# Expert layer: the second token tile takes half of its experts by fetched rows and VectorE additions

## The chip, the cores and the metric

The kernel is one program on one core of a Trainium2 chip. The metric is the device time of one launch in microseconds, the median of the runs shown. The profile is one more execution, recorded by the hardware profiler.

## The reference, cut to what matters

A model of one token sequence (256 tokens, 2048 features, everything float32): a block with a recurrent and a sparse-attention branch, then an expert layer, then two more layers. The change touches the expert layer alone:

```
s = q . sub_keys                       # 8 heads, two halves of 128 keys each
s1, i1 = top_k(s[0], 16); s2, i2 = top_k(s[1], 16)
top_s, pos = top_k(all 256 sums s1 + s2, 16)        # 16 experts a head, 128 a token
eid = i1 * 128 + i2                    # one of 16384 experts
gate = softmax(top_s)
act = gelu(x . expert_u[eid])
out = sum over the token's 128 experts of gate * act * expert_v[eid]
```

Each expert has a row u and a row v of 2048 numbers. A token uses 128 of the 16384.

## The kernel before, in words

**Weights.** All weights of the program come through one stream of units of 128x2048 float32 (1 MB), which SyncE loads into a ring of four slots (`ring`). ScalarE rounds each unit to `hi_w` in two halves (`split_hi`, L216 and L217), and VectorE or GpSimd subtracts to get `lo_w` (`split_lo`, L222 and L224), so that a float32 product becomes three fast ones (hi.hi, hi.lo, lo.hi) on TensorE. A slot is loaded again when TensorE has used its unit (semaphore `unit_used`).

**Dense evaluation.** The layer doesn't pick experts. It evaluates all 16384 for all 256 tokens, 128 experts to a unit: all those with the same second index i2. A u unit (`u_unit`) gives 128 experts x 256 tokens into a PSUM bank (16 steps of three 256-column products), ScalarE takes gelu of it into `GG`. A dense table G of gates (zero where a token doesn't use an expert) is multiplied in, and a v unit (`v_unit`) multiplies the result, again split in hi and lo (`high`, L2212, and `low`, L2392), by v: for two token tiles of 128 and four column blocks of 512, three products each, 24 matmuls of 512 columns (L2074), summed over all units in PSUM.

**Order.** The experts go in two halves of 64 units: u0, v0, u1, v1. For each half x is rebuilt and added to (`x_added`, L2511). In u1 a paired form is used for 60 of the 64 units: one 512-column product for hi_w with both halves of x (L2043) and one of 256 columns (L2045), which VectorE sums (`u_sum`, L2348) ahead of gelu.

**The gate table.** In units 0 to 36 of u0 VectorE finds the 16 best of each list; from unit 40 on, 32 bursts of TensorE (`burst`, L2059) build G for 8 tokens each out of one-hot tables, which VectorE builds (`build`, L2356 and L2357) and ScalarE scales (`gate`, L2217). One half of a burst's result is multiplied into `GG` (`product`), the other is staged to memory (`stage`, tensor `other_G`) and read back in u1 (`load_back`, `product_back`).

**Who splits.** GpSimd does `split_lo` for the first 40 units of u0 and nothing else in this layer; VectorE does all the others. The order on every engine is written out by hand, as program text of that engine; SyncE's queue carries the stream, the table and the saved x in one order.

Of the kernel before, what the change touches and what calls it, by code (L numbers as in the profile page):

```python
# [13 lines left out]
P = 128  # L14
# [38 lines left out]
STREAM = [("w_in", 19), ("br_b", 2), ("br_a", 2), ("w_out", 4), ("wq", 4), ("u0", 16), ("v0", 16), ("u1", 16), ("v1", 16),  # L53
# [6 lines left out]
GROUPS = _g  # L60

# [9 lines left out]
def constants():  # L71
# [10 lines left out]
    c["iota"] = f(t)  # L82
    c["anti"] = f(u + t == P - 1)
# [32 lines left out]
def build(nc, dram, consts):  # L116
# [1786 lines left out]
    HK = PK // 2  # L1903
# [3 lines left out]
    GG = sb("GG", (P, T, HK))  # L1907
# [18 lines left out]
    gg = lambda i: GG[:, :, i]  # L1926
# [4 lines left out]
    other_G = scratch("other_G", (P, T, HK))  # L1931
    back = [h[:].rearrange("p a q c -> p (a q c)").rearrange("p (n i) -> p n i", i=HK) for h in (hot1, hot2)]
    kept = x[:].rearrange("p t d -> p (t d)")
# [9 lines left out]
    W0, A0 = GROUP["u0"] * SLOTS, GROUP["a_in"] * SLOTS  # L1943
    EARLY = 3
    tile = lambda tt: slice(tt * P, (tt + 1) * P)
    V_ORDER = ([(tt, c) for tt in range(NT) for c in range(4)], [(tt, c) for c in range(4) for tt in range(NT)])
    NB, NK = T // 8, T // 32
    U_AT, V_AT = (0, 2 * HK), (HK, 3 * HK)
    ROUTED, STEADY = 37, (36, 48)
    AT = [40 * KC + 364 * j // NB for j in range(NB)]  # L1950
    AT_UNIT = [at // KC for at in AT]
    PAIRED = HK - SLOTS
    at_unit = lambda i: [j for j in range(NB) if AT_UNIT[j] == i]
    AT_CHUNK = [48 + 2 * k for k in range(NK)]
    LATE = [[], []]
    for hf, (marks, n) in enumerate(((AT_UNIT, 8), (AT_CHUNK, 32))):
        at = 0
        for m in marks:
            LATE[hf].append((m, at))
            at += n * (HK - m)  # L1960
        assert at <= NT * D

    def rest(hf, j):

        (m, at), n = LATE[hf][j], (8, 32)[hf]
        return m, kept[:, at:at + n * (HK - m)].rearrange("p (n i) -> p n i", n=n)

    with nc.Block() as block:  # L1968
        @block.sync
        def _(sp):  # L1970
# [8 lines left out]
            cload(sp, iota[:], "iota", S("sk_in"))  # L1979
            sp.dma_start(x_saved, x[:]).then_inc(S("x_out"), 16)  # L1980
# [4 lines left out]
            def refill_unit(w):  # L1985
                g, s = divmod(w, SLOTS)
                sp.wait_ge(S("unit_used"), W0 + w + 1)
                sp.dma_start(ring[s][:], wst[GROUP["u0"] * SLOTS + SLOTS + w]).then_inc(S(f"landed{s}"), 16)

            def load_back(k):  # L1990
                sp.dma_start(back[k % 2], other_G[:, 32 * k:32 * k + 32, :]).then_inc(S(f"back{k % 2}"), 16)

            u0, v0 = GROUP["u0"], GROUP["v0"]
            refill(u0, STEADY[0] // SLOTS)
            for i in range(STEADY[0], HK):
                refill_unit(i)
                for j in at_unit(i):
                    sp.wait_ge(S("staged"), j + 1)
                    sp.dma_start(other_G[:, 8 * j:8 * j + 8, :], staged[:, j % 2]).then_inc(S(f"other_out{j % 2}"), 16)
            refill(v0, 4)  # L2000
            sp.wait_ge(S("late"), NB)
            sp.dma_start(x[:], x_saved).then_inc(S("x_again"), 16)
            refill(v0 + 4, 12)
            u1, v1 = GROUP["u1"], GROUP["v1"]
            refill(u1, 2)
            sp.wait_ge(S("x_added"), 8)
            sp.dma_start(x_saved, x[:]).then_inc(S("x_out"), 16)
            refill(u1 + 2, STEADY[1] // SLOTS - 4)
            for p in range(2):
                sp.wait_ge(S(f"other_out{p}"), 16 * (NB // 2))  # L2010
            load_back(0)
            refill(u1 + STEADY[1] // SLOTS - 2, 1)
            load_back(1)
            refill(u1 + STEADY[1] // SLOTS - 1, 1)
            for i in range(STEADY[1], HK):
                refill_unit(2 * HK + i)
                if i in AT_CHUNK[:NK - 2]:
                    k = AT_CHUNK.index(i)
                    sp.wait_ge(S("back_used"), k + 1)
                    load_back(k + 2)  # L2020
            refill(v1, 4)
            sp.wait_ge(S("late"), NB + NK)
            sp.dma_start(x[:], x_saved).then_inc(S("x_again"), 16)
            for dst, name in ((gcol[:], "a_norm_w"), (gcol2[:], "norm_final_w")):
                sp.dma_start(dst, dram[name]).then_inc(S("xa_col"), 16)
            sp.wait_ge(S("back_used"), NK)
            sp.dma_start(fgain[:], bcast("norm_final_g")).then_inc(S("fgain"), 16)
            refill(v1 + 4, 12)
# [5 lines left out]
        def _(t):  # L2034
            def u_unit(g, s, hf, paired, between=()):
                t.wait_ge(S("gelu_free"), g * 4 + (hf * HK + s + 1))
                t.wait_ge(S(f"lo{s}"), g + (GROUP[f"u{hf}"] + 1))
                for k in range(KC):
# [3 lines left out]
                    if paired:  # L2042
                        nc.tensor.matmul(PS[:, s, :].rearrange("p (a c) -> p a c", a=2), hi_w[s][:, k * P:(k + 1) * P], both_x[:, :, k, :],  # L2043
                                         start=k == 0, stop=False)
                        m = nc.tensor.matmul(PS[:, s, 0:T], lo_w[s][:, k * P:(k + 1) * P], hi_x[:, k, :], start=False, stop=k == KC - 1)  # L2045
                        continue
# [1665 lines left out]
```

## Time and profile before

| what | us |
|---|---|
| median of 3 runs (3487.63 to 3488.38) | 3488.04 |
| span of the profiled execution, first to last instruction | 3487.5 |
| TensorE busy in it | 3450.4 (99%) |
| VectorE busy | 2194.8 (63%) |
| ScalarE busy | 1766.6 (51%) |
| GpSimd busy | 347.2 (10%) |
| first and last product of the expert layer (u0 to v1) | 924.5 to 2424.5 |

Busy time is the union of an engine's instructions. Matmuls are pipelined, so a matmul's duration (0.39 us for 512 columns) is longer than the distance of two starts (0.23 us); what a unit costs is read from starts. Engines in rows: PE is TensorE, PEld its weight loads, DVE VectorE, ACT ScalarE, POOL GpSimd, SP SyncE; a q behind the name is that engine's sequencer.

### The profile page before, as it was taken

Reading aid. Unit: us, or ns where it says so; the run is one execution under the profiler, and the core shown is the slowest. Engines: PE = TensorE matmul, PEld = TensorE weight load, DVE = VectorE, ACT = ScalarE, POOL = GpSimd, SP = SyncE. Lnnn points to the kernel's source line nnn. Section 1 sums busy time; section 2 is a strip of 40 time slices with the busy share of each in tenths; the row PEclk is TensorE's granted clock in tenths of the full one; section 3 lists DMA queues with packets and bytes.
Section 4 is the critical chain, followed back from the end, with each engine's and each line's share of the span. In section 5 each row is a group of like instructions: output and inputs, shape, how many; then the busy total and the mean of one; then the engine's idle time right before and its main releaser. Section 6 shows DMA issues by size and latency. Waiting matters only on the chain. (4 is left out here: it accounts for less than half of the span.)

```text
span 3487.5 us, 50169 instructions
## 1 busy us (share of the span) xinstructions
PE 3450.4 (99%) x20098; PEld 2893.0 (83%) x20098; DVE 2194.8 (63%) x2937; ACT 1766.6 (51%) x2613; POOL 347.2 (10%) x215
## 2 busy tenths in 40 slices
PE   8999999999999999999999999999999999999999
PEld 7777777787999998888888888887788877788887
DVE  4777765765666686555555565555788885555454
ACT  5563444334444785444444444444655654444863
POOL 0000000000499100000000000000122210000000
PEclk9999999999999999999999999999999999999999
DMA  6554533565445555555555666555543435455444
GB/s 235 203 198 156 174 138 130 187 232 212 161 183 182 174 168 183 215 190 185 191 213 184 240 231 228 189 185 180 191 148 138 148 140 202 168 194 190 145 150 164
DMA packets 111214, 638.58 MB, mean 183 GB/s; under 512 B 17770, under 2 KB 23690, under 8 KB 39224
## 3 DMA queue, kind: packets, MB, share of 16 engines
q1 hardware_dynamic: 106696, 622.98, 50.0%
q0 software_dynamic: 4336, 13.14, 1.2%
q8 instruction: 119, 1.95, 0.2%
q14 instruction: 63, 0.52, 0.0%
HBM read 611.10 MB, written 21.54 MB: 181 GB/s over the span
## 5 line engine op out<-in xcount | busy, mean ns | idle before, releaser
L222 DVE TENSOR_TENSOR lo_w<-ring,hi_w 128x1024 fp32r<-128x1024 f32 x500 | 612.4, 1225 | 862.7 <-ACT hi_w L216 854.2
L216 ACT CAST hi_w<-ring 128x1024 fp32r<-128x1024 f32 x540 | 567.1, 1050 | 946.3 <-DMA ring<-in_wstream 920.6
L224 DVE TENSOR_TENSOR lo_w<-ring,hi_w 128x1024 fp32r<-128x1024 f32 x500 | 612.4, 1225 | 0.0
L217 ACT CAST hi_w<-ring 128x1024 fp32r<-128x1024 f32 x540 | 564.4, 1045 | 0.0
L639 PE MATMUL PS<-hi_w,both_x 128*128 128x512 f32 (+2 forms) x1520 | 500.2, 399 | 4.9 <-DVE RKV L1651 3.0
L2074 PE MATMUL PS<-hi_w,hi_g 128*128 128x512 f32 x1024 | 404.0, 395 | 2.0 <-issue 2.0
L2667 PE MATMUL PS<-hi_w,both_x 128*128 128x512 f32 x1232 | 401.3, 401 | 4.1 <-PEq L1968 1.9
L2074 PE MATMUL PS<-lo_w,hi_g 128*128 128x512 f32 x1024 | 403.4, 394 | 0.0
L2074 PE MATMUL PS<-hi_w,lo_g 128*128 128x512 f32 x1024 | 403.2, 394 | 0.0
L2048 PE MATMUL PS<-both_x,hi_w 128*128 128x256 f32 x2176 | 390.5, 281 | 3.1 <-POOL lo_w L224 3.1
L639 PEld LDWEIGHTS PS<-hi_w,both_x 128*128 128x128 f32 x1520 | 285.2, 189 | 78.3 <-issue 12.3
L2048 PEld LDWEIGHTS PS<-both_x,hi_w 128*128 128x128 f32 x2176 | 334.9, 189 | 3.5 <-ACT GG L2291 3.4
L2043 PE MATMUL PS<-both_x,hi_w 128*128 128x512 f32 x960 | 336.0, 393 | 0.0
L2048 PE MATMUL PS<-both_x,lo_w 128*128 128x256 f32 x1088 | 307.1, 282 | 0.0
L639 PE MATMUL PS<-lo_w,both_x 128*128 128x512 f32 (+2 forms) x760 | 293.1, 386 | 0.0
L2667 PEld LDWEIGHTS PS<-hi_w,both_x 128*128 128x128 f32 x1232 | 231.9, 188 | 61.2 <-DVE x L3035 2.8
L2045 PE MATMUL PS<-both_x,lo_w 128*128 128x256 f32 x960 | 270.5, 282 | 0.0
L3182 PE MATMUL PS<-hi_w,both_x 128*128 128x512 f32 x768 | 247.4, 398 | 0.0
L2667 PE MATMUL PS<-lo_w,both_x 128*128 128x512 f32 x616 | 241.4, 392 | 0.0
L2074 PEld LDWEIGHTS PS<-hi_w,hi_g 128*128 128x128 f32 x1024 | 192.7, 188 | 46.7 <-issue 2.2
L2074 PEld LDWEIGHTS PS<-hi_w,lo_g 128*128 128x128 f32 x1024 | 192.1, 188 | 45.8
L2074 PEld LDWEIGHTS PS<-lo_w,hi_g 128*128 128x128 f32 x1024 | 192.1, 188 | 44.3
(579 smaller groups left out, 5272.4 us busy)
## 6 DMA issues: line engine op xcount, KB each, us to landing
ring<-in_wstream SPq DMA_DIRECT2D x540, 1024.0 KB, 4.8
other_G<-staged SPq DMA_DIRECT2D x32, 256.0 KB, 6.0
hot<-other_G SPq DMA_DIRECT2D x8, 1024.0 KB, 7.0
gates_dram<-gst POOLq DMA_DIRECT2D x8, 512.0 KB, 4.6
x_dram<-x SPq DMA_DIRECT2D x2, 2048.0 KB, 11.8
x<-x_dram SPq DMA_DIRECT2D x2, 2048.0 KB, 9.3
prev<-RKV POOLq DMA_DIRECT2D x6, 508.0 KB, 5.1
x<-in_x SPq DMA_DIRECT2D x4, 512.0 KB, 8.9
```

The costliest lines, as they stand in the source:

```text
L216: a.copy(hi_w[s][:, 0:HALF], ring[s][:, 0:HALF]).then_inc(S(f"hi{s}"), 1)
L217: a.copy(hi_w[s][:, HALF:UNIT], ring[s][:, HALF:UNIT]).then_inc(S(f"hi{s}"), 1)
L222: v.tensor_tensor(lo_w[s][:, 0:HALF], ring[s][:, 0:HALF], hi_w[s][:, 0:HALF].bitcast(F32), ALU.subtract)
L224: v.tensor_tensor(lo_w[s][:, HALF:UNIT], ring[s][:, HALF:UNIT], hi_w[s][:, HALF:UNIT].bitcast(F32), ALU.subtract)\
L639: mm = nc.tensor.matmul(PS[:, bank(m, tt), 0:n], xa[:, xo + kk_, tt * P:(tt + 1) * P], wa[slot][:, k * 512:k * 512 + n], start=(kk_ == 0 a ...
L2043: nc.tensor.matmul(PS[:, s, :].rearrange("p (a c) -> p a c", a=2), hi_w[s][:, k * P:(k + 1) * P], both_x[:, :, k, :], start=k == 0, stop=F ...
L2045: m = nc.tensor.matmul(PS[:, s, 0:T], lo_w[s][:, k * P:(k + 1) * P], hi_x[:, k, :], start=False, stop=k == KC - 1)
L2048: m = nc.tensor.matmul(PS[:, s, 0:T], wa[s][:, k * P:(k + 1) * P], xa[:, k, :], start=(k == 0 and p == 0), stop=(k == KC - 1 and p == 2))
L2074: m = nc.tensor.matmul(PS[:, 4 * tt + c, :], ga[:, s, tt * P:(tt + 1) * P], wa[s][:, c * 512:(c + 1) * 512], start=first and p == 0, stop= ...
L2667: mm = nc.tensor.matmul(o, xa[:, kk, tt * P:(tt + 1) * P], wa[q][:, k * 512:(k + 1) * 512], start=(kk == 0 and p == 0), stop=(kk == KC - 1 ...
L3182: mm = nc.tensor.matmul(PS[:, 2 * (m % 2) + tt, :], xa[:, kk, tt * P:(tt + 1) * P], wa[q][:, k * 512:(k + 1) * 512], start=(kk == 0 and p ...
```

## The change

- The stream is reordered: 64 u units (`u_b`, i2 below 64), 64 u units (`u_a`), then 128 v units. All 128 u units use the form with three 256-column products.
- Token tile 0 goes as before. Token tile 1 uses dense products for the 64 expert blocks of `u_a` only. For the blocks of `u_b` its 128 selected experts are taken one slot at a time: GpSimd fetches by indirect DMA, for each of the 128 tokens, the 8 KB row of v of its expert in slot s (`fetch`, out-of-range indices, those of the other half, are skipped), and VectorE adds row times weight to x (`add_row`, 128x2048, with a drain). The activation of that expert and token is fetched by 128 more indirect DMAs of one element per token (`cell`), out of a copy of all activations of `u_b` in memory (`act_dram`, written by SyncE in `keep_act`).
- So 64 v units are dense (24 matmuls, `v_dense`) and 64 are half (12 matmuls, tile 0 alone, `v_half`): six dense, then half and dense in turn, then six half (`v_expert`).
- 54 additions stand in `u_a` (one a unit from the tenth on), 74 in the first 119 of the 128 v units. Rows go through three or four buffers; a fetch waits until the addition that used its buffer is done.
- GpSimd does `split_lo` for all 64 units of `u_b` and for every second unit of v; VectorE for `u_a` and for the other half of v. In `u_a` GpSimd issues 128 cells and its fetches.
- VectorE's products with `GG` (`product`, `late`, `product_back`, `u_sum`) go; in their place come `copied`, `times_a` (128x256, one a unit of `u_a`) and `times_b` (128x128, one a half unit). The table for `u_b` is loaded in one DMA of 4 MB ahead of the refills of the v units.

```
+HK = PK // 2
+LEAD = 6
+def v_expert(p):
+    if p < LEAD:
+        return False, p
+    if p >= 2 * HK - LEAD:
+        return True, p - HK
+    k = (p - LEAD) // 2
+    return ((p - LEAD) % 2 == 0, k) if (p - LEAD) % 2 == 0 else (False, LEAD + k)
...
+    ADD0, ADDS_U = 10, HK - 10
+    ADDS_V = PK - ADDS_U
+    SPAN_V = LAST_A - 2
+    adds_u = lambda i: [i - ADD0] if i >= ADD0 else []
...
+    fetch_tick = {s: add_tick[row_before[s]] + 1 if row_before[s] >= 0 else (ADD0 if s < 3 else add_tick[s] - 6) for s in range(PK)}
...
+            def keep_act(w):
+                s = w % SLOTS
+                sp.wait_ge(S("gelu_free"), w + 5)
+                sp.dma_start(act_dram[w], act_stage(w)).then_inc(S(f"act_out{s}"), 16)
...
+            sp.dma_start(tab_b, other_G).then_inc(S("tab_in"), 16)
+            for p in range(VB):
+                refill_unit(VB + p)
+                sparse, k = v_expert(p)
+                if sparse and k + AHEAD < HK:
+                    load_act(k + AHEAD)
...
+            def v_half(g, s, last=False):
+
+                t.wait_ge(S(f"lo{s}"), g + (GROUP["v"] + 1))
+                t.wait_ge(S("g_lo"), g * 4 + (s + 1))
+                for c in range(4):
+                    m = v_products(g, s, 0, c, False, last)
...
+            for p in range(VB):
+                if p + 2 < VB:
+                    high(p + 2)
+                hi(VB + p + SLOTS - 1)
...
         @block.gpsimd
         def _(g):
-            for w in range(AT_UNIT[0]):
+            def fetch(s):
+
+                n = row_of[s]
+                if row_before[s] >= 0:
+                    g.wait_ge(S("added"), row_before[s] + 1)
...
+                g.indirect_dma_start(rows[n], None, dram["v_rows"], bass.IndirectOffsetOnAxis(ap=row_at[:, s:s + 1], axis=0),
+                                     bounds_check=HK * P - 1, oob_is_err=False).then_inc(S(f"row_{n}"), 16)
+
+            def cell(s):
+
+                g.indirect_dma_start(raw[:, s:s + 1], None, act_cells, bass.IndirectOffsetOnAxis(ap=cell_at[:, s:s + 1], axis=0),
+                                     bounds_check=HK * P * T - 1, oob_is_err=False).then_inc(S(f"cells{s // CELLS}"), 16)
...
+            for w in range(HK):
+                lo(w)
+                if w == 48:
+                    g.wait_ge(S("row_at"), 1)
+                    fetch(0)
+            for s in (1, 2):
+                fetch(s)
+            for s in range(SLOTS):
+                g.wait_ge(S(f"act_out{s}"), 16 * (HK // SLOTS))
+            for s in range(2 * CELLS):
+                cell(s)
+            for i in range(ADD0, HK):
+                for s in fetches(i):
+                    fetch(s)
+                at = 2 * CELLS + 4 * (i - ADD0)
+                for s in range(at, min(at + 4, PK)):
+                    cell(s)
+            lo(VB)
+            lo(VB + 2)
+            for p in range(VB):
+                for s in fetches(HK + p):
+                    fetch(s)
+                if p % 2 and p + SLOTS - 1 < VB:
+                    lo(VB + p + SLOTS - 1)
...
+            def add_row(s):
+
+                n = row_of[s]
+                if s == 0:
+                    v.wait_ge(S("x_again"), 16)
+                v.wait_ge(S(f"row_{n}"), 16 * row_turn[s])
+                v.scalar_tensor_tensor(out=x1, in0=rows[n], scalar=weight[:, s:s + 1], in1=x1, op0=ALU.mult, op1=ALU.add)
+                v.drain().then_inc(S("added"), 1)
...
+            for i in range(HK):
+                lo(HK + i + SLOTS - 2)
+                if i:
+                    times_a(i - 1)
+                if i in (9, 12, 36, 38):
+                    weigh((9, 12, 36, 38).index(i))
+                for s in adds_u(i):
+                    add_row(s)
...
+            for p in range(VB):
+                if p + 3 < VB and v_expert(p + 3)[0]:
+                    times_b(v_expert(p + 3)[1])
+                    v.drain()
+                if p + 2 < VB:
+                    low(p + 2)
+                if p < VB - 1:
+                    lo(VB + p + SLOTS - 1)
+                for s in adds_v(p):
+                    add_row(s)
```

## Rows read from the trace of the kernel before

**Rows 1.** Stages u0 (two parts), v0, u1, v1: busy time of each engine.
```profile
core 0: us, PE busy (x) PEld busy (x) DVE busy (x) ACT busy (x) POOL busy (x), PEclk, DMA share, GB/s
924.50:1155.00 230.50, 227.45 (x1921) 227.05 (x1920) 149.49 (x419) 107.34 (x138) 200.15 (x76) 1.00 0.50 178
1155.00:1353.80 198.80, 196.90 (x1697) 196.70 (x1695) 151.63 (x176) 156.49 (x360) 0.00 (x0) 1.00 0.53 175
1353.80:1709.60 355.80, 355.67 (x1535) 288.37 (x1536) 194.66 (x231) 161.63 (x190) 0.00 (x0) 1.00 0.54 194
1709.60:2068.60 359.00, 359.00 (x2114) 319.12 (x2113) 211.49 (x211) 170.74 (x193) 0.00 (x0) 1.00 0.59 217
2068.60:2424.50 355.90, 355.90 (x1539) 288.45 (x1538) 190.34 (x204) 163.70 (x192) 0.00 (x0) 1.00 0.55 198
```

**Rows 2.** Waits of 924 to 2430 us: who waited for whom, total, times, longest.
```profile
DVE lo_w L222 <- ACT hi_w L216: 425.4, 180, 8.0
ACT hi_w L216 <- DMA ring<-in_wstream: 392.6, 129, 8.3
...
PE PS L2048 <- POOL lo_w L224: 3.1, 2, 1.6
```

**Rows 3.** Timeline of TensorE: start, us, line; a u unit without and with pairing.
```profile
924.74 0.40 PE L2048 MATMUL PS<-both_x,hi_w 128*128 128x256 f32 x2
...
930.40 1.04 PE L2113 MATMUL PS<-ident,Q 128*128 128x128 f32 x8
...
1709.85 0.39 PE L2043 MATMUL PS<-both_x,hi_w 128*128 128x512 f32 x1
...
2045.84 0.40 PE L2048 MATMUL PS<-both_x,hi_w 128*128 128x256 f32 x2
```

**Rows 4.** Groups of instructions: VectorE, GpSimd and ScalarE, with count, busy and mean ns.
```profile
L216 ACT CAST hi_w<-ring 128x1024 fp32r<-128x1024 f32 x257 | 270.0, 1051 | 392.6 <-DMA ring<-in_wstream 392.6
...
L2356 DVE TENSOR_TENSOR hot<-iota,R 128x1024 f32<-128x1024 f32 x32 | 39.0, 1219 | 30.2 <-ACTq L2301 30.1
...
L2986 DVE TENSOR_TENSOR AS<-AM 128x128 f32<-128x128 f32 x32 | 14.7, 459 | 2.5
...
L2544 DVE SCALAR_TENSOR_TENSOR x<-x,rstat,hot 128x2048 f32<-128x2048 f32 x2 | 4.7, 2351 | 0.2
...
L1426 DVE TENSOR_TENSOR prob<-prob,pen 128x256 f32<-128x256 f32 x8 | 3.4, 426 | 0.9
```

**Rows 5.** Timeline of VectorE in v0: one unit's subtraction, two halves.
```profile
1449.35 1.23 DVE L222 TENSOR_TENSOR lo_w<-ring,hi_w 128x1024 fp32r<-128x1024 f32 x1 [2.93 <-ACT hi_w L216]
...
1450.49 1.22 DVE L224 TENSOR_TENSOR lo_w<-ring,hi_w 128x1024 fp32r<-128x1024 f32 x1
```

**Rows 6.** Timelines of GpSimd, then VectorE, over the same stretch of u0.
```profile
980.09 2.41 POOL L222 TENSOR_TENSOR lo_w<-ring,hi_w 128x1024 fp32r<-128x1024 f32 x1 [0.88 <-ACT hi_w L216]
982.46 4.46 POOL L224 TENSOR_TENSOR lo_w<-ring,hi_w 128x1024 fp32r<-128x1024 f32 x1
986.88 4.47 POOL L222 TENSOR_TENSOR lo_w<-ring,hi_w 128x1024 fp32r<-128x1024 f32 x1
...
980.28 4.37 DVE L2460 TENSOR_TENSOR hot<-ppf,iota 128x2048 f32<-128x2048 f32 x1
984.72 4.35 DVE L2463 TENSOR_TENSOR hot<-hot,idf 128x2048 f32<-128x2048 f32 x1
989.14 2.29 DVE L2465 TENSOR_REDUCE route<-hot 128x128 f32<-128x2048 f32 x1
```

**Rows 7.** DMA issues with KB and us to landing; GpSimd's own issue instructions.
```profile
ring<-in_wstream SPq DMA_DIRECT2D x257, 1024.0 KB, 4.8
...
L1336 POOL DMA_DIRECT2D TC<-T_dram x4 | 3.8, 940 | 11.4 <-DMA T_dram<-Xs 11.4
L1303 POOL DMA_DIRECT2D prev<-RKV x6 | 3.3, 542 | 5.9 <-ACTq L1041 5.9
```

**Rows 8.** The stretch with the highest DMA rate of those asked (columns of rows 1).
```profile
2000.00:2050.00 50.00, 50.00 (x300) 44.56 (x299) 36.42 (x37) 24.05 (x27) 0.00 (x0) 1.00 0.77 290
```

More of the change, by code:

```diff
@@ new lines, in build @@
+    G0_FROM, X0_UNTIL = ADDS_U + 12, PK - 16
+    row_of, row_turn, row_before, last = {}, {}, {}, {"x0": -1, "h1": -1, "h2": -1}
+    turns = {n: 0 for n in rows}
+    for s in range(PK):
+        if s == G0_FROM:
+            last["g0"] = -1
+        if s == X0_UNTIL:
+            x0_done = last.pop("x0")
+        n = min(last, key=lambda k: (last[k], k != "x0", k))
+        turns[n] += 1
+        row_of[s], row_turn[s], row_before[s], last[n] = n, turns[n], last[n], s
+    fetch_tick = {s: add_tick[row_before[s]] + 1 if row_before[s] >= 0 else (ADD0 if s < 3 else add_tick[s] - 6) for s in range(PK)}
@@ L1968, in build @@
+    fetches = lambda tick: [s for s in range(3, PK) if fetch_tick[s] == tick]
+    assert all(fetch_tick[s] < add_tick[s] for s in range(3, PK)) and sorted(add_tick) == list(range(PK))
+    X0_BACK = add_tick[x0_done] - HK + 3
+    CELLS = 32
     with nc.Block() as block:
@@ L1987, in refill_unit @@
                 sp.wait_ge(S("unit_used"), W0 + w + 1)
[L1988 to L1995, printed above, removed]
+                sp.dma_start(ring[s][:], wst[W0 + SLOTS + w]).then_inc(S(f"landed{s}"), 16)
@@ L1996, in _ @@
+            for i in range(STEADY, HK):
                 refill_unit(i)
+                keep_act(i)
                 for j in at_unit(i):
[L1998 to L2004, printed above, removed]
@@ L2021, in _ @@
[L2021 to L2028, printed above, removed]
+                    if j < NB0:
+                        sp.wait_ge(S("staged"), j + 1)
+                        sp.dma_start(other_G[:, 8 * j:8 * j + 8, :], staged[:, j % 2]).then_inc(S(f"other_out{j % 2}"), 16)
@@ L2077, in v_unit @@
+            def v_half(g, s, last=False):
+                t.wait_ge(S(f"lo{s}"), g + (GROUP["v"] + 1))
+                t.wait_ge(S("g_lo"), g * 4 + (s + 1))
+                for c in range(4):
+                    m = v_products(g, s, 0, c, False, last)
+                    if last and c < 3:
                         m.then_inc(S("v_bank"), 1)
@@ new lines, in _ @@
+            places()
+            for i in range(ROUTED, HK):
+                for j in at_unit(i):
+                    copied(j)
+                    if j + 2 < NB:
+                        build(j + 2)
+            lo(HK)
+            lo(HK + 1)
+            for i in range(HK):
[6 more added lines that the diff above has]
+                    add_row(s)
+                if i == HK - 1:
+                    v.drain()
+                    v.wait_ge(S("other_out0"), 8 * NB0)
+                    v.wait_ge(S("other_out1"), 8 * NB0)
+                    low(0)
+                    low(1)
```

406 lines of the change are left out of this document (204 added, 202 removed).

## The prediction

> **What bounds the kernel now.** The stages of the expert layer, read first, show TensorE without a gap: 355.67 of 355.8 us in v0, all of u1 and v1, and 424.35 of 429.3 in u0, at a granted clock of 1.00, the upper of its two levels (2.4 GHz) [rows 1]. The view of waits agrees: over these 1500 us TensorE waits 3.1 us for a split, while ScalarE waits 392.6 us for units of the ring and VectorE 425.4 us for ScalarE [rows 2]. So the layer costs what its matmuls cost, and its other engines have room: VectorE is busy 55% in v0 and v1, ScalarE 46%, the DMA engines 55%, GpSimd not at all after unit 40. The change takes matmuls away and spends this room. The question is whether the room can be spent by several engines at once, and the timelines of GpSimd and VectorE answer it [rows 6].
>
> **Part 1, matmuls taken away.** v0 and v1 take 355.8 + 355.9 = 711.7 us for 128 units, 5.56 us each [rows 1]. After, 64 units have 24 matmuls and 64 have 12: TensorE needs 64 x 5.56 + 64 x 2.78 = 534 us, 178 less. The 60 paired u units start every (2045.84 - 1709.85) / 60 = 5.60 us; an unpaired one takes 930.40 - 924.74 = 5.66 [rows 3]. That costs 60 x 0.06 = 4 us.
>
> **Part 2, the port.** A VectorE product of two SBUF tensors (128x2048, started at 980.28) [rows 6] runs 4.37 us, and its twin 4.35; the reduction of the same size with one input, right after, runs 2.29 beside a working GpSimd. GpSimd's halves of `split_lo`, 2.41 us, take 4.46 and 4.47 beside the two products. The ends tell how: GpSimd ends at 982.50, VectorE 2.15 later, GpSimd at 986.92, which is 2.27 later, VectorE at 989.07. Each waits until the other is through: strict turns. Now list what has two SBUF inputs in the new v stage, with the price of each:
> - GpSimd `split_lo` of 64 units: 128 halves x 2.27 = 291 us.
> - VectorE `split_lo` of the other 64: 128 halves x 1.14 (distance of the two starts [rows 5]) = 146 us.
> - 74 row additions: 74 x 2.35, the nearest form being the scalar_tensor_tensor of 128x2048 [rows 4] = 174 us. The drain after each is taken as covered by the overlap of starts.
> - `low` of 64 dense units, 128x256, at 0.43 each, and of 64 half units and `times_b` 64 times, both 128x128. 0.46 stands for 128x128 and 0.43 for twice that [rows 4], so I take 0.38, between that and nothing: 28 + 49 = 77 us.
>
> In turns this is 291 + 146 + 174 + 77 = 688 us. At a hand-over the waiting instruction loses 0.13 us less than alone (2.15 against 2.28), 128 times: 17 us. That leaves 671. Some time neither engine works: the first units, the last six half units, and where GpSimd, held by a fetch that waits for an addition, comes late with its split. I take 14 us, a tenth of a microsecond a unit. The v stage is then 685 us, not 534: of the 178 us taken from TensorE, 27 stay.
>
> ScalarE is not the bound: 128 units x 2.1 (two halves of 1.05 [rows 4]) and 128 roundings of `high` are under 350 us. DMA moves in this stage 128 units (134 MB), 74 fetches of about half of 128 rows of 8 KB (39 MB), the 4.2 MB table and 4.2 MB of activations, 181 MB. At 685 us that is 265 GB/s; the trace shows 290 GB/s at a share of 0.77 [rows 8], so it fits, and it wouldn't fit in 534 us at that rate (626 us). The Trainium skill, DMA: Bandwidth & Descriptors, Specifications, puts HBM's limit for a core at about 358 GB/s; by it 181 MB would take an estimated 507 us and DMA would bound nothing. No run here reaches that rate.
>
> **Part 3, the u units.** In units 40 to 63 GpSimd now splits beside the one-hot builds. The stretch is 198.8 us for 24 units [rows 1], 8.3 each. GpSimd needs 24 x 2 x 2.37 (starts 980.09 and 982.46 [rows 6]) = 114 us of turns, the 64 builds 64 x 1.22 = 78 [rows 4]: 192 of 198.8. It fits on paper and will slip: I take 4 us, bounds 0 and 30. In `u_a` VectorE has per unit 2.28 (split) + 0.43 (`times_a`) + 2.35 = 5.1 of 5.66 us, with GpSimd splitting nothing: 0. The 128 cells and the fetches are GpSimd's. The trace has no indirect DMA; its direct ones hold GpSimd 0.54 to 0.94 us each [rows 7]. I take 0.9, as every row's address is computed: 67 of them ahead of the tenth unit are 60 us, and `weigh` of the second 32 stands in tick 12, 12 x 5.66 = 68 us in. Bounds 0.54 and twice the upper row, 1.9. SyncE's 64 stores of activations wait for a gelu that ends about 1 us after the unit it has already waited for: 0. The 4.2 MB table stands in SyncE's queue ahead of the refill for v unit 4, which has four dense units, 22 us, while 4.2 MB at 290 GB/s are 14 and one ring unit lands in 4.8 [rows 7]: 3 us, bounds 0 and 10. Routing work moved nowhere; `places` and four `weigh` are a few small instructions in VectorE's slack.
>
> **Sum.** 711.7 - 685 = 27 gained; 4 + 4 + 3 = 11 given back: 16 us less. The profiled execution (span 3487.5) stands 0.5 under the median of the runs, so 3488 - 16 = **3472 us**. What a measurement of this kernel can tell from no change is about 0.2%, 7 us.
>
> **Rivals.** *TensorE stays the bound, wholly or half.* Then v is 534 us and the time 3488 - 178 + 11 = 3321. For it: each engine's own busy sum fits (VectorE 397 of 534, GpSimd 291 plus fetches). Against it: the turns [rows 6], without exception there. Half way, where splits fall into VectorE's pauses, is about 3400. Chance 0.14.
>
> *GpSimd's descriptor work decides, slower.* `weigh` stands in VectorE's program ahead of the splits for the next units, and in `u_a` all of TensorE's lo_w come from VectorE. If an indirect DMA costs c, 67 c + 6 us must be under 68 us plus the 5 us by which splits run ahead: it decides from c = 1.0. At c = 1.4: 67 x 1.4 + 6 - 73 = 27 us, and then 16 ticks with five DMAs each, 7.0 against 5.66, 21 us. Total 48 us more: 3472 + 48 = 3520. For it: each needs 128 addresses read from SBUF, which by the turns of [rows 6] may also have to wait for VectorE's two-input instructions. Against it: the direct ones stay [rows 7] under 1 us. The Trainium skill, DMA: Bandwidth & Descriptors, SWDGE vs HWDGE vs iDMA, says that VectorE's 2-port mode locks GpSimd out of writing descriptors; by that rule alone the additions, which have two inputs, would not. No row shows it. Chance 0.27.
>
> *The loop of a slot gets too long, slower.* A dense unit's slot: its own 5.56, landing 4.8 (6 in this traffic), 2.1 for hi, 2.3 for lo with two turns of GpSimd 4.5, an addition standing ahead of `low` in six of ten ticks 1.4, `times_b` and `low` 1.0 with a turn 1.1: 24 us for two pairs, 12.0 a pair of a half and a dense unit where TensorE needs 8.3. The 58 pairs are 696, six dense units 33, six half ones 23: 752 less what overlaps when turns are fewer, some 20. v is 732, 20 more than before: 3488 + 20 + 11 = 3519, up to 3540. It decides above 11.3 us a pair. For it: the order of VectorE's program, fixed. Against it: as long as VectorE is never idle, its sum bounds and the loop is inside it. Chance 0.17.
>
> **Numbers.** The serialised port within its own bounds, 3440 to 3505, has 0.42; it holds faster 0.34, same 0.06, slower 0.02. TensorE-bound 0.14, all faster. Descriptors 0.27: slower 0.24, same 0.02, faster 0.01. Slot loop 0.17: slower 0.15, same 0.02. Faster 0.49, same 0.10, slower 0.41. The range 3400 to 3550 leaves out 0.1 below and under 0.1 above (c of 1.9 would give over 3580).
>
> **What would show it.** GpSimd's `split_lo` in the v stage with durations near 4.4 us beside additions, and additions near 4.5 us beside GpSimd, prove the turns; a stage of 685 us, TensorE busy about 78% in it, waiting for lo_w and for lo_g. In `u_a` TensorE at 5.66 us a unit and VectorE never waiting for cells; if VectorE waits there, the descriptors decide. ScalarE waiting for the ring in the v stage beyond its present 3 us a unit would speak for the slot loop or DMA. I am wrong if additions run at 2.35 beside GpSimd, or if TensorE's pauses bring its granted clock down, at which every matmul would take longer; no row here shows the lower level.

## The result, and the profile of the kernel after

The changed kernel takes 3581.8 us (median of four runs, 3581.58 to 3584.34), the kernel before 3488.2 beside it: ratio 1.0263, 95% interval 1.0249 to 1.0278. It is 2.6% slower. The forecast was 3472 us, faster, in a range of 3400 to 3550.

The profiled execution spans 3582.6 us, 95.1 more than before. TensorE is busy 3364.7 us (94%), VectorE 2500.4 (70%), ScalarE 1687.9 (47%), GpSimd 1146.6 (32%). The expert layer by stages, which answer to [rows 1] (stages `u_b`, `u_a`, v, and all behind them):

```profile
core 0: us, PE busy (x) PEld busy (x) DVE busy (x) ACT busy (x) POOL busy (x), PEclk, DMA share, GB/s
924.50:1372.00 447.50, 435.49 (x3677) 433.71 (x3676) 312.80 (x522) 245.44 (x482) 338.59 (x128) 0.99 0.54 187
1372.00:1800.30 428.30, 373.29 (x3014) 370.57 (x3013) 297.58 (x247) 149.09 (x196) 246.05 (x185) 0.94 0.63 223
1800.30:2516.40 716.10, 601.51 (x2304) 465.83 (x2304) 590.54 (x398) 284.94 (x376) 414.98 (x197) 0.92 0.68 249
2516.40:3582.60 1066.20, 1048.41 (x5631) 855.28 (x5630) 697.70 (x827) 581.89 (x956) 99.52 (x63) 1.00 0.45 164
```

TensorE had hardly a gap in these stages before; now it has them in all three, and its granted clock is 0.94 in `u_a` and 0.92 in v. The gelu of each unit marks a finer border than these windows, since it follows its unit in every kernel. ScalarE's timeline, last gelu of `u_b` and of `u_a`, and below it the last of u0 in the kernel before:

```profile
1365.13 0.39 ACT L2354 ACTIVATE act_late<-PS 128x256 f32<-128x256 f32 x1 [3.38 <-PE PS L2095]
1792.96 0.38 ACT L2354 ACTIVATE act_late<-PS 128x256 f32<-128x256 f32 x1 [1.95 <-PE PS L2095]
```
```profile
1351.94 0.60 ACT L2291 ACTIVATE GG<-PS 128x256 f32<-128x256 f32 x1 [2.12 <-PE PS L2048]
```

By these borders the first u stage is 440.6 us against 427.4 (+13), the second 427.8 against 359.0 of u1 [rows 1] (+69). The v stage, from the last gelu to its last product, is 723.4 against 713.6, both v stages before with the 1.9 us ahead of v0 (+10). What follows the layer is 3 us longer. 13 + 69 + 10 + 3 = 95. So the saved matmuls brought nothing, and `u_a` lost most. Some of the waits from 924 to 2530 us, which answer to [rows 2]:

```profile
POOL hot L2408 <- DVEq L2497: 225.4, 51, 8.3
ACT hi_g L2276 <- DVE R L2510: 190.6, 49, 9.4
PE PS L2114 <- DVE lo_g L2517: 111.4, 45, 6.0
PE PS L2095 <- DVE lo_w L239: 47.6, 13, 19.2
DVE route L2487 <- DMA raw<-act_dram,cell_at: 28.0, 2, 26.8
PE PS L2107 <- issue: 7.8, 4, 5.7
PE PS L2114 <- issue: 7.4, 1, 7.4
```

In v TensorE waits 111.4 us for `low`. In `u_a` it waits 47.6 us for VectorE's lo_w, up to 19.2 at a time, and VectorE had waited 26.8 us in one piece for cells. This second wait is where to look first. VectorE's timeline at the first two `weigh` (L2487), at the first addition, and at an addition after the long wait:

```profile
1421.30 0.19 DVE L2487 TENSOR_TENSOR route<-route,raw 128x32 f32<-128x32 f32 x1 [1.24 <-DMA raw<-act_dram,cell_at]
1425.63 2.35 DVE L2496 SCALAR_TENSOR_TENSOR x<-x,route 128x2048 f32<-128x2048 f32 x1
...
1463.81 0.19 DVE L2487 TENSOR_TENSOR route<-route,raw 128x32 f32<-128x32 f32 x1 [26.79 <-DMA raw<-act_dram,cell_at]
1474.96 2.35 DVE L2496 SCALAR_TENSOR_TENSOR x<-x,route 128x2048 f32<-128x2048 f32 x1 [5.71 <-DMA x<-in_v_rows,row_at]
```

GpSimd's timeline of the cells: the first, one beside an addition of VectorE, and two with VectorE still:

```profile
1371.38 1.00 POOL L2413 DMA_INDIRECT raw<-act_dram,cell_at  x1 [12.67 <-DMA act_dram<-act_late]
1426.88 1.96 POOL L2413 DMA_INDIRECT raw<-act_dram,cell_at  x1 [0.30 <-issue]
1440.79 0.99 POOL L2413 DMA_INDIRECT raw<-act_dram,cell_at  x1 [0.30 <-issue]
1442.09 1.00 POOL L2413 DMA_INDIRECT raw<-act_dram,cell_at  x1 [0.30 <-issue]
```

Even with VectorE idle two starts are 1.30 us apart. The first 64 cells take from 1371.4 to 1463.9: 1.44 us each. The cell at 1426.88 started under the addition of 1425.63, took 1.96 us and ended 0.86 us behind it. This repeats: 19 indirect transfers of `u_a` start under an addition, and every one ends 0.85 to 0.88 us behind that addition. The longest starts right behind the start of the addition of 1464.08 (2.35 us):

```profile
1464.18 3.12 POOL L2413 DMA_INDIRECT raw<-act_dram,cell_at  x1 [0.30 <-issue]
```

So a transfer waits for the end of the addition under which it was issued, and then works on. All indirect transfers of `u_a` as groups; the fetches, which wait for an addition to free their buffer and so stand near the next one, cost more than the cells (the third group, fetches into `x`, has 18 with a mean of 1656 ns):

```profile
L2413 POOL DMA_INDIRECT raw<-act_dram,cell_at x128 | 154.3, 1206 | 51.4 <-issue 38.7 <-DMA act_dram<-act_late 12.7
L2408 POOL DMA_INDIRECT hot<-in_v_rows,row_at x35 | 53.2, 1519 | 90.4 <-DVEq L2497 81.7 <-issue 8.7
```

In the v stage the turns can be seen. GpSimd, then VectorE, over the same 8 us:

```profile
2102.77 2.49 POOL L237 TENSOR_TENSOR lo_w<-ring,hi_w 128x1024 fp32r<-128x1024 f32 x1
2105.21 2.55 POOL L239 TENSOR_TENSOR lo_w<-ring,hi_w 128x1024 fp32r<-128x1024 f32 x1
```
```profile
2102.92 2.58 DVE L2510 TENSOR_TENSOR R<-R,both_x 128x128 f32<-128x128 f32 x1
2105.60 2.45 DVE L2517 TENSOR_TENSOR lo_g<-GG,hi_g 128x256 fp32r<-128x256 f32 x1
2107.97 2.34 DVE L2496 SCALAR_TENSOR_TENSOR x<-GG,route,x 128x2048 f32<-128x2048 f32 x1
```

A product of 128x128 takes 2.58 us because it started 0.15 us behind a half of GpSimd's split; the next half makes `low` wait in the same way. `low` is what TensorE waits for in this stage, 111.4 us in 45 waits, though not at the one shown. The other way round GpSimd waits for an addition. GpSimd, then VectorE:

```profile
2130.11 3.61 POOL L237 TENSOR_TENSOR lo_w<-ring,hi_w 128x1024 fp32r<-128x1024 f32 x1
```
```profile
2129.12 2.34 DVE L2496 SCALAR_TENSOR_TENSOR x<-hot,route,x 128x2048 f32<-128x2048 f32 x1
```

The half of a split, 2.41 us alone, started 0.99 us behind the addition and ended 2.26 us behind its end. VectorE's groups from 1830 to 2400 us (the other two addition groups also have 2341 and 2342 ns):

```profile
L237 DVE TENSOR_TENSOR lo_w<-ring,hi_w 128x1024 fp32r<-128x1024 f32 x51 | 108.6, 2130 | 77.5 <-ACT hi_w L231 77.5
L2496 DVE SCALAR_TENSOR_TENSOR x<-hot,route,x 128x2048 f32<-128x2048 f32 x34 | 79.6, 2342 | 0.0
L2517 DVE TENSOR_TENSOR lo_g<-R,hi_g 128x128 fp32r<-128x128 f32 x50 | 63.6, 1272 | 6.1 <-ACT hi_g L2276 2.7
L239 DVE TENSOR_TENSOR lo_w<-ring,hi_w 128x1024 fp32r<-128x1024 f32 x51 | 62.0, 1215 | 0.0
L2510 DVE TENSOR_TENSOR R<-R,both_x 128x128 f32<-128x128 f32 x51 | 56.3, 1104 | 4.0
L2517 DVE TENSOR_TENSOR lo_g<-GG,hi_g 128x256 fp32r<-128x256 f32 x50 | 55.1, 1101 | 5.1 <-issue 0.4
```

The additions are not lengthened here (in the whole stage one of 74 is, to 4.49 us); the first halves of splits and the small products are. Laying VectorE's and GpSimd's split intervals of the v stage over each other gives the port sum: VectorE busy 590.5, GpSimd's splits 321.4, at least one of them 662, neither 54 of the 716 us. The prediction's prices, each engine alone, added up to 671, so the two saved next to nothing by running at the same time.

### The profile page after: what moved, and what is told of

It reads as the page before. It is cut to its first block and busy times, and to the rows that moved or that the text cites. A ratio compares the mean times of both kernels' runs of the same rounds, so it can differ in the third digit from the quotient of the medians.

```text
span 3582.6 us, 51470 instructions
## 1 busy us (share of the span) xinstructions
PE 3364.7 (94%) x20290; PEld 2841.7 (79%) x20290; DVE 2500.4 (70%) x2870; ACT 1687.9 (47%) x2597; POOL 1146.6 (32%) x647
## 5 line engine op out<-in xcount | busy, mean ns | idle before, releaser
L237 DVE TENSOR_TENSOR lo_w<-ring,hi_w 128x1024 fp32r<-128x1024 f32 x412 | 561.0, 1362 | 592.2 <-ACT hi_w L231 581.2
L2095 PE MATMUL PS<-both_x,hi_w 128*128 128x256 f32 x4096 | 746.5, 284 | 51.7 <-DVE lo_w L239 47.6
L2095 PEld LDWEIGHTS PS<-both_x,hi_w 128*128 128x128 f32 x4096 | 643.0, 192 | 54.9 <-issue 38.8
L2095 PE MATMUL PS<-both_x,lo_w 128*128 128x256 f32 x2048 | 584.9, 286 | 0.0
L239 DVE TENSOR_TENSOR lo_w<-ring,hi_w 128x1024 fp32r<-128x1024 f32 x412 | 509.3, 1236 | 0.0
L237 POOL TENSOR_TENSOR lo_w<-ring,hi_w 128x1024 fp32r<-128x1024 f32 x128 | 345.6, 2700 | 367.5 <-ACT hi_w L231 365.4
L2114 PE MATMUL PS<-hi_w,hi_g 128*128 128x512 f32 x768 | 332.5, 433 | 122.0 <-DVE lo_g L2517 111.4
L2095 PEld LDWEIGHTS PS<-both_x,lo_w 128*128 128x128 f32 x2048 | 391.5, 191 | 0.0
L654 PEld LDWEIGHTS PS<-hi_w,both_x 128*128 128x128 f32 x1520 | 284.5, 189 | 79.4 <-issue 12.3
L239 POOL TENSOR_TENSOR lo_w<-ring,hi_w 128x1024 fp32r<-128x1024 f32 x128 | 334.5, 2613 | 0.0
L2114 PE MATMUL PS<-lo_w,hi_g 128*128 128x512 f32 x768 | 323.1, 421 | 0.0
L2114 PE MATMUL PS<-hi_w,lo_g 128*128 128x512 f32 x768 | 321.1, 418 | 0.0
L2114 PEld LDWEIGHTS PS<-hi_w,hi_g 128*128 128x128 f32 x768 | 157.1, 205 | 183.9 <-DVE lo_g L2517 124.4
L2496 DVE SCALAR_TENSOR_TENSOR x<-hot,route,x 128x2048 f32<-128x2048 f32 x77 | 182.7, 2373 | 33.4 <-DMA hot<-in_v_rows,row_at 33.2
```

What stands on the lines that cost most here:

```text
L237: v.tensor_tensor(lo_w[s][:, 0:HALF], ring[s][:, 0:HALF], hi_w[s][:, 0:HALF].bitcast(F32), ALU.subtract)
L239: v.tensor_tensor(lo_w[s][:, HALF:UNIT], ring[s][:, HALF:UNIT], hi_w[s][:, HALF:UNIT].bitcast(F32), ALU.subtract)\
L654: mm = nc.tensor.matmul(PS[:, bank(m, tt), 0:n], xa[:, xo + kk_, tt * P:(tt + 1) * P], wa[slot][:, k * 512:k * 512 + n], start=(kk_ == 0 a ...
L2095: m = nc.tensor.matmul(PS[:, s, 0:T], wa[s][:, k * P:(k + 1) * P], xa[:, k, :], start=(k == 0 and p == 0), stop=(k == KC - 1 and p == 2))
L2114: m = nc.tensor.matmul(PS[:, 4 * tt + c, :], ga[:, s, tt * P:(tt + 1) * P], wa[s][:, c * 512:(c + 1) * 512], start=first and p == 0, stop= ...
L2496: v.scalar_tensor_tensor(out=x1, in0=rows[n], scalar=weight[:, s:s + 1], in1=x1, op0=ALU.mult, op1=ALU.add)
```

## The experiments

Two theories stood after these rows. For `u_a`: GpSimd's indirect transfers come too late for `weigh`. Rival: VectorE's own load with additions is too much. For v: turns between GpSimd's splits and VectorE. Rivals: the traffic of the row fetches, or the additions alone. "One execution" beside an experiment says that its time is that of its profile alone; differences of a few us between two such times mean nothing. The kernel before took 3494.39 (one execution) beside the first four, and 3490.95 (3488.39 to 3494.02) beside the next four, all eight on one chip.

**Fewer cells up front** (one execution). Each `weigh` needs 32 cells, but only the first `weigh` is needed at the tenth unit.

```
-            for s in range(2 * CELLS):
+            for s in range(CELLS + 4):
...
-                at = 2 * CELLS + 4 * (i - ADD0)
-                for s in range(at, min(at + 4, PK)):
+                at = CELLS + 4 + 2 * (i - ADD0)
+                for s in range(at, min(at + 2, PK)):
...
-                if i in (9, 12, 36, 38):
+                if i in (10, 30, 50, 62):
```

> The changed kernel with its 128 element fetches spread: 36 ahead of the first addition and two a unit after that, in place of 64 and four, and each group of weights multiplied in later. Theory (an indirect DMA holds GpSimd 1.3 to 1.4 us, and VectorE, waiting for it, delays lo_w in u_a): the wait of 26.8 us for the second group and the waits for rows after it go, TensorE waits under 5 us in u_a in place of 47.6, and with the clock back at its upper level u_a takes some 368 us in place of 421; the whole falls by 50 to 65 us, to about 3520 to 3530. Rival (u_a is slow for its DMA traffic or for the row additions themselves): the waits only move to other instructions and the whole falls by less than 20 us.

3511.02 us, 73 less than the changed kernel in its profiled execution, somewhat more than the 50 to 65 expected. TensorE in `u_a`, which answers to the 428 us above:

```profile
1372.00:1430.00 58.00, 58.00 (x495) 58.00 (x494) 30.89 (x35) 22.68 (x30) 42.70 (x39) 1.00 0.59 198
1430.00:1500.00 70.00, 70.00 (x597) 70.00 (x596) 61.27 (x49) 28.26 (x38) 58.72 (x38) 1.00 0.81 276
1500.00:1600.00 100.00, 100.00 (x852) 100.00 (x851) 88.09 (x73) 39.77 (x53) 83.26 (x54) 1.00 0.81 274
```

No gap, clock 1.00, VectorE busy 88% with the same splits and additions. The stage takes 361.8 us by its gelus (1363.27 to 1725.08), 64 x 5.65. The rival falls: VectorE has time for all of it, if nothing holds it up. The same number of transfers is sent; only when they have to be there differs. The same kernel was run again later, for an interval.

> The cells edit alone, again, for an interval: 3511 us by one look, 73 below the changed kernel. If the pauses of TensorE's instruction stream go with the burst of 36 cells alone, some executions should show them here as well, and be up to 20 us longer; if not, all lie within 3505 to 3515.

3518.11 us (3514.12 to 3522.27, four runs, another chip), a little above the 3505 to 3515 expected, ratio to the kernel before 1.0082 (1.0066 to 1.0097): still 0.8% slower than before, by the v stage (715.5 us). `u_a` took 361.8 us again, and no pause of TensorE's own stands in it.

**All splits of v by VectorE** (one execution). GpSimd keeps only the fetches.

```
-            lo(VB)
-            lo(VB + 2)
...
-                if p % 2 and p + SLOTS - 1 < VB:
-                    lo(VB + p + SLOTS - 1)
...
-                if HK <= w < VB or VB <= w < 2 * VB and w % 2 or 2 * VB <= w < 2 * VB + SLOTS:
+                if HK <= w < 2 * VB + SLOTS:
...
+            lo(VB + 2)
```

> The changed kernel with all lo_w of the v stage made by VectorE, none by GpSimd. Theory (VectorE and GpSimd take strict turns on instructions with two SBUF inputs): VectorE's own work is 128 x 2.28 + 74 x 2.35 + 77 = 543 us plus drains, so the v stage falls from 716 to 560 to 600 us although VectorE has more to do, and additions take 2.35 us each; the whole is about 3440. Rival (the loop of a slot, DMA landing, rounding, split, is what is too long, or DMA is): the v stage stays above 690 us, since traffic and order are the same. Second rival (VectorE is simply full): giving it 64 more splits makes the stage longer than 716.

3487.92 us: 96 less than the changed kernel, although VectorE got 128 more halves of splits. That is about the time of the kernel before, and a miss: 3440 with a v stage of 560 to 600 us was expected. The v stage and three of its groups:

```profile
1795.70:2420.60 624.90, 566.17 (x2304) 447.41 (x2304) 528.02 (x524) 287.57 (x378) 89.77 (x72) 0.95 0.79 289
```
```profile
L2513 DVE TENSOR_TENSOR lo_g<-GG,hi_g 128x256 fp32r<-128x256 f32 x55 | 23.4, 425 | 5.4
L2506 DVE TENSOR_TENSOR R<-R,both_x 128x128 f32<-128x128 f32 x55 | 21.1, 383 | 4.4
L2513 DVE TENSOR_TENSOR lo_g<-R,hi_g 128x128 fp32r<-128x128 f32 x55 | 15.9, 289 | 4.0 <-issue 0.5
```

The small products fall from 1.10 to 1.27 us to 0.29 to 0.43; VectorE does more work in 62 us less busy time. The stage is 625 us and not nearer to TensorE's 534: ScalarE still waits 277.9 us for units of the ring, and TensorE 58.6 for lo_g. `u_a` was left alone and repeats its loss (428.8 us, 49.4 of waiting for lo_w). In the cells edit `u_a` was mended and v was not (712.4 us): the loss of `u_a` and that of v are independent.

**Without the row fetches of v** (one execution; the v stage doesn't fetch its rows, the additions take what lies in the buffers).

```
-                for s in fetches(HK + p):
-                    fetch(s)
```

> The changed kernel without the row fetches of the v stage: the 74 additions are made of whatever the buffers hold, so tile 1 gets wrong rows; everything else stays. Theory (turns on the port): 39 MB of traffic and 71 indirect DMAs less change little, the v stage stays at 680 to 716 us. Rival (DMA traffic or GpSimd's descriptor work is the bound): it falls under 640.

3597.18 us, longer than the changed kernel, and its v stage is longer than what theory (680 to 716 us) and rival (under 640) expected. The v stage and GpSimd's and VectorE's heaviest groups:

```profile
1801.80:2530.20 728.40, 602.40 (x2304) 473.74 (x2304) 626.15 (x398) 284.98 (x376) 387.63 (x124) 0.89 0.52 192
```
```profile
L2495 DVE SCALAR_TENSOR_TENSOR x<-hot,route,x 128x2048 f32<-128x2048 f32 x31 | 98.3, 3171 | 0.0
L2509 DVE TENSOR_TENSOR R<-R,both_x 128x128 f32<-128x128 f32 x47 | 86.1, 1832 | 3.7
```
```profile
L239 POOL TENSOR_TENSOR lo_w<-ring,hi_w 128x1024 fp32r<-128x1024 f32 x48 | 156.1, 3251 | 0.0
```

The DMA share falls from 0.68 to 0.52 and 72 indirect transfers are gone from GpSimd, yet the stage is 12 us longer. So traffic and descriptors alone don't set the pace of v in the changed kernel. This kernel can't say that they cost nothing, as the turns fall elsewhere in it. Without a fetch in the way GpSimd starts its splits as soon as hi_w is there, and they fall beside the additions, which now wait too (3.17 against 2.34 us).

**Without the additions of v** (one execution; the 74 row additions of the v stage are left out, their waits and fetches stay).

> The changed kernel without the 74 additions of the v stage (their waits, drains and all fetches stay), so tile 1 lacks those experts. Theory (turns): what is left in turns is 291 + 146 + 77 = 514 us, under TensorE's 534, so the v stage falls to 540 to 600 us with the same DMA traffic. Rival (DMA or slot loop): with all traffic kept it stays above 660.

3488.43 us, v 608.9 us (540 to 600 expected), VectorE busy 416 in it, DMA at 291 GB/s. VectorE's group that TensorE waits for is longer than ever, with a mean that says that nearly every `low` of a half unit falls into a turn of GpSimd:

```profile
L2518 DVE TENSOR_TENSOR lo_g<-R,hi_g 128x128 fp32r<-128x128 f32 x57 | 152.6, 2677 | 72.9 <-ACT hi_g L2276 71.5
```

Taking 174 us of additions away brings 107. What a turn costs in the last two kernels thus seems to depend on where it falls, not on its length alone; no run moved a turn without changing something else.

**The same two cuts without turns** (one execution each): all splits of v by VectorE, and once no fetches, once no additions in v.

> e2_split_dve without the row fetches of the v stage (additions of what the buffers hold, so tile 1 gets wrong rows). Its v stage took 625 us where TensorE needs 534, at 289 GB/s. If ring units landing late are what is left (traffic): the stage falls under 590 and ScalarE's wait for the ring falls from 278 us. If VectorE's own work is (543 us plus drains, in a fixed order): it stays above 605.

> e2_split_dve without the 74 additions of the v stage (waits, drains and fetches stay, tile 1 lacks those experts). VectorE's own work falls to 369 us. If VectorE is what is left: the stage falls to 535 to 570. If traffic is: it stays above 600, as 182 MB at the 290 GB/s so far seen are 626 us.

v takes 573 us without fetches and 555 without additions, against 625 with both. Both are as expected if traffic and VectorE's work count. Now the fetches are worth 52 us (ScalarE's wait for the ring falls from 277.9 to 192.9), and the additions 70. The second has the highest rate of the study:

```profile
1820.30:2375.20 554.90, 541.90 (x2304) 431.64 (x2304) 364.94 (x450) 285.41 (x380) 79.32 (x72) 1.00 0.88 326
```

The whole programs took 3456.02 and 3442.02; their `u_a` is the unmended one, and by TensorE's waits it lost still more there (below).

**Both edits, then a third.** First the cells edit and the splits edit together (one execution), then with them units 40 to 63 of `u_b` split by VectorE, so that GpSimd is out of the way of the one-hot builds (five executions):

```
-            for w in range(HK):
+            for w in range(AT_UNIT[0]):
                 lo(w)
...
-            lo(HK)
-            lo(HK + 1)
+                lo(i + SLOTS - 2)
```

> The same without the edit of units 40 to 63: 3410 to 3425, the difference to e6_all being the price of GpSimd's splits beside the one-hot builds. I take 18 us by the stage times (429 before, 447 after), my prediction had 4; under 6 us would say that the 18 have another cause.

> The changed kernel with three edits: element fetches spread as in e1_cells, all lo_w of the v stage by VectorE as in e2_split_dve, and lo_w of units 40 to 63 of u_b by VectorE as in the kernel before. If the losses are separate places of one program they add up: 73 us (e1_cells) and 97 us (e2_split_dve) under the changed kernel's 3583, and the 18 us that the first 64 u units had become longer go back: 3395 to 3410, faster than both kernels. Rival (relieving one place only moves the wait to the next): above 3450.

The first gave 3425.38, the second 3432.54 (3421.61 to 3441.47), ratio 0.9823 (0.9802 to 0.9845): 1.8% faster than the kernel before, though the 3395 to 3410 expected were missed. The third edit does what it should in its own stage: the last gelu of `u_b` comes at 1354.0 in place of 1363.9, 2 us from the kernel before. But the total is no better, since `u_a` took 393.7 us, and 386.6 in the kernel with two edits, where the cells edit alone has 361.8. Four us out of the middle of the stretch, and TensorE's waits from 1395 to 1432 us, kernel with two edits:

```profile
1414.00:1418.00 4.00, 3.04 (x12) 2.66 (x12) 0.00 (x0) 0.00 (x0) 2.99 (x3) 0.50 0.02 0
```
```profile
PE PS L2095 <- issue: 9.0, 21, 1.0
```

TensorE waits for no other engine here: VectorE and ScalarE stand still, DMA is idle at a share of 0.02, only GpSimd sends its burst of cells. TensorE starts 12 matmuls in 4 us where 34 are usual (852 in 100 us, above), and its granted clock drops to 0.50, the lower of its levels (1.2 GHz). The waits named issue sum to 16.2 us in the kernel with three edits, and to 38.1 and 45.6 in the two kernels of the section above, which have the burst of 64. But a burst isn't enough: the changed kernel and the first four experiments have it too, of 64 or 36 cells, and not one such wait in `u_a`. Nor do the pauses keep step with the transfers: from 1405 to 1428 us they end 1.4 or 0.7 us apart (once 2.9), where GpSimd's transfers start 1.30 apart.

**The burst let out four at a time.**

```
             for s in range(CELLS + 4):
+                if s % 4 == 0:
+                    g.wait_ge(S("unit_used"), W0 + HK + s // 4)
                 cell(s)
```

It ran on top of two edits, beside a repetition of the two edits as they were; and, because those two agreed, on top of three, beside a repetition of the three.

> Both earlier edits (cells of two experts fewer up front, all splits of the v stage by VectorE), and the first 36 cell transfers are let out four at a time behind the product units of the u stage of the first tile instead of in one burst. The number: in the kernels with both edits TensorE issued late just in the burst (9.0 us in 21 pauses of L2095 in the kernel with cells and splits, 16.2 in the one with all three edits, 38.1 and 45.6 in the two variants of the split kernel), its matmuls came one at a time and the granted clock fell to 0.5, so that this stage took some 20 us more than with the cells edit alone. Theory: it is the back-to-back stream of indirect transfers that holds TensorE's own instruction stream back; spread out, the pauses go and the time is 3400 to 3412 us. Rival one: the pauses are a chance of where the engine's code is fetched, whatever GpSimd does: then the time stays at 3420 to 3440 and pauses of 9 to 16 us still stand in that stage. Rival two: the spread cells keep GpSimd late for the first row fetches, TensorE then waits for VectorE after unit 10: 3430 or more, with waits for lo_w.

> The kernel with cells and splits edited, again, for an interval and a second look at its stage of the first tile's u units. By the first look 3425 us; with pauses of TensorE between 0 and 16 us in the burst of cells the executions should lie between 3405 and 3440, and if the pauses come by chance the second profile shows another sum than 9.0 us.

> All three edits (fewer cells up front, all splits of the v stage by VectorE, the splits of u units 40 to 63 by VectorE), and the first 36 cells let out four at a time behind the product units. By stages: the u stage of the second half ends at 1354 instead of 1364 (seen in the kernel with the three edits), and without pauses of TensorE's own issue the next stage takes 362 to 364 us and v 604 to 618. Theory one, the burst of 36 indirect transfers causes the pauses: 3398 to 3406, and no waits named issue for L2095. Theory two, the pauses come with the u stage's edit or with the chip and the moment, not with the burst: 3420 to 3440 as that kernel had, with 10 us or more of such waits.

> The kernel with the three edits again, with its burst of 36 cells, on the chip and in the hour of the one above. Theory one: 3420 or more, with pauses. If it comes at 3398 to 3406 without pauses too, they belong to the moment and nothing was shown about the burst.

| kernel | us (runs) | ratio to before, 95% | issue waits of L2095 | `u_a` |
|---|---|---|---|---|
| two edits, spread | 3413.1 (3400.9 to 3416.3) | 0.9765 (0.9748 to 0.9782) | none | 364.1 |
| two edits, again | 3409.5 (3406.1 to 3416.1) | 0.9775 (0.9760 to 0.9790) | none | 361.8 |
| three edits, spread | 3411.9 (3405.5 to 3421.0) | 0.9774 (0.9756 to 0.9792) | 3.0 | 372.8 |
| three edits, again | 3432.2 (3421.5 to 3444.0) | 0.9830 (0.9804 to 0.9857) | 12.3 | 390.2 |

The first two rows are of another chip than the first execution of the two edits, the last two of the same. With two edits the pauses of the first execution didn't come back, burst or not, so the expected 3400 to 3412 would have shown nothing; whether the chip, the moment or chance took them away is open. With three edits they stand in all three profiled executions, and spreading the burst took the time down by 20 us, with intervals that don't touch. The 3411.9 lie between the two theories, 3398 to 3406 and 3420 to 3440:

```profile
PE PS L2095 <- issue: 3.0, 10, 0.6
```
```profile
PE PS L2095 <- issue: 12.3, 20, 1.8
```

(From 1350 to 1430 us, three edits spread, three edits again.) The burst makes the pauses longer; it isn't all of their cause, as 3.0 us stay without it, at the same place of the program. That they are TensorE's own instructions coming late is one guess (nothing else that it could wait for is named), and the trace doesn't bear it out. It lists two queues that carry instructions. The busier one moves nothing from 1376 to 1690 us in any kernel, with pauses or without, and neither moves anything from 1396 to 1431 in the kernel with two edits, where these are all the queues at work:

```profile
q1 hardware_dynamic: 432, 3.15, 25.1%
q0 software_dynamic: 768, 0.01, 1.6%
```

## Why the prediction was wrong

**Part 3, `u_a`: 0. This step failed, by 65 us, the largest part of the miss.** It alone would have turned the sign of the forecast, and so would part 2 below: with the cells edit alone the kernel is still 0.8% slower. The price of an indirect transfer on GpSimd was taken as 0.9 us, nearest to the direct ones of [rows 7]. It is 1.30 from start to start with VectorE still and 1.44 in the mean over the first 64. The rival on descriptor work had the condition (from 1.0) and, at 1.4, its price: 27 us for the second `weigh` and 21 for the ticks behind it, 48. TensorE's waits sum to 47.6. That the sum fits so well is partly luck: 19.2 us are the first wait, at the second `weigh` (VectorE stood 26.8), and 28.4 the twelve behind it, since a transfer issued under an addition takes up to 3.12 us. But these 48 weren't all. The stage lost 69 us, of which 3 are the unpaired units (361.8 without waits against 359.0) and 48 the waits; the other 18 are matmuls that ran longer, at the lower granted clock that the waits brought:

```profile
1430.00:1500.00 70.00, 43.74 (x321) 43.02 (x320) 27.48 (x24) 15.85 (x21) 55.98 (x47) 0.80 0.39 137
```

The last sentence of the prediction named this and priced it nowhere. The argument for the rival was the better one: an indirect transfer, which reads its 128 indices out of SBUF, is held up by VectorE's additions, in 19 of 19 cases until 0.85 to 0.88 us behind the addition. That the reading of indices is what waits is argued, not shown. The Trainium skill, SBUF — State Buffer, Who interferes with whom, has the rule that a VectorE instruction with two SBUF inputs contends with a GpSimd instruction that reads SBUF; the 19 transfers, which read their indices there, agree with it, and not with the narrower rule that the prediction weighed, by which additions would not disturb them.

**Part 2, the port: the turns right, one term off.** The sum of turns, overlaps taken off, was 671 us; measured, at least one of the two engines is in its work for 662. What failed is the last term, the time in which neither works: 14 taken, 54 measured. Together 716.0 in place of 685, and the 27 us of gain were gone. VectorE's order is fixed, and 77.5 us of its idle time from 1830 to 2400 ended with ScalarE's hi_w, which waits for the ring or behind hi_g: this looks like the loop of a slot, which stood as a rival with 732 us, nearer to 716 than the 685 are (its six half units stand at 23 us without a reason; at 2.78 each they are 17, and the sum 726). Its own sign is missing: ScalarE waits for the ring 235.3 us in the v stage, 1.8 a unit, not over 3. It waits 190.6 us more for `times_b` (hi_g <- R), which turns delay. So how much of the 54 us is the loop's is open. That the turns are real is what the rows show, in both directions, and moving all splits to VectorE: more work on VectorE, 91 us less for the stage.

The signature was half wrong. The prediction looked for additions and GpSimd splits of 4.4 us, and called itself wrong if additions ran at 2.35 beside GpSimd. They did, 73 of 74 of them, and the turns are there all the same: an addition that starts first is not lengthened, GpSimd's half beside it is (3.6 in place of 2.4 us, 14 times from 1860 on, in a like place of the program). By their order additions mostly follow on small products that have already waited; without the fetches they didn't, and took 3.17 in the mean. The turns were paid by instructions of 0.3 to 0.4 us, by first halves of splits and by GpSimd. `low`, one of the small ones, is what TensorE waits for.

**Part 3, `u_b`: 4 us taken, bounds 0 to 30; measured 13.** The one-hot builds went from 1.22 to 1.93 and 1.99 us (means of L2456 and L2457 in the last 24 units), and TensorE stood 7.8 us in front of bursts (L2107, 5.7 of them at once, at 1175.66). Moving GpSimd out of these units gave back 10. A term that the prediction put at nothing, the stores of activations, is in it: the first copy of a burst's result waits until 40 of them have landed, and VectorE stood 8.0 us for that just ahead of TensorE's 5.7. With the third edit the two are 4.8 and 1.8; what the stores cost alone is not shown.

**DMA, the table, the matmuls.** DMA was not seen to bound the changed kernel (without the fetches its v stage was no shorter), and 326 GB/s at a share of 0.88 is possible where 290 [rows 8] was the highest seen. The unpaired units cost what was said. TensorE-bound v (534 us) was never reached: the best v stage with all its work took 604 us.

Accounts: forecast -16, measured +95. Of the 111 between them `u_a` has 65, v 34 (31 of it the stage, the rest a late start), `u_b` 9, and 3 lie behind the layer.

## What to carry to other kernels

Before work is given to an idle engine, list which of its instructions exclude whom, and look at what the other engine has next: a 0.3 us product that TensorE needs, behind a 2.4 us split, is the turn that shows. An indirect transfer costs the issuing engine time of its own; a batch of them has a due time, and here it was cheaper to send first only what is needed first. Splitting on VectorE alone and sending fewer cells up front turned 2.6% slower into 2.2% faster. An idle TensorE costs its clock too, so waits of 48 us had a price of 66.

## What the runs showed of the hardware

- An indirect DMA of 128 elements or rows occupies GpSimd 0.99 to 1.00 us plus a gap of 0.30 at best. In the mean cells take 1.2 and fetches 1.5 to 1.7 in `u_a` of the changed kernel. Issued under a two-input VectorE instruction of 2.35 us, it ends 0.85 to 0.88 us behind it (19 of 19), so it takes up to 3.12.
- The granted clock falls in stages with waits: v of the changed kernel, with 111.4 us of waits for `low`, none over 6.0, has 0.92 in the mean, and `u_a`, with 47.6 us for lo_w, one of 19.2, has 0.94. In the stages without gaps it is 1.00.
- TensorE can pause with no other engine named while GpSimd sends indirect transfers: 3 to 46 us in six of the fourteen profiles of kernels that send them, nothing in the eight others. The kernel with two edits has 9.0 us in one profile and none in the other, on another chip. The cause is open. The Trainium skill, Runtime: NRT & Kernel Launch, Instruction fetch mechanics, describes instructions as fetched ahead by a DMA queue of the sequencer, mostly hidden. No run here shows that this is what pauses, and under the pauses of the kernel with two edits no packet of an instruction queue moved.
- DMA moved 326 GB/s at a share of 0.88 over 555 us, rows of 8 KB fetched by index included.
